# Head outputs turned inside the next weight block, and the first weight block of the heads rounded by two engines

## The reference, cut to what matters

```python
xn = rmsnorm(x, g_attn_norm)
z = einsum('bsd,de->bse', xn, w_in)           # queries, keys, values, gates of all branches
h_a, C, n, m = mlstm_branch(...)              # 8 heads, 128 query/key and 256 value channels each
h_b = attend(q_b, c_kv, k_rope)               # latent attention over 8 x 1024 cached rows
merged = sigmoid(gate_a) * (h_a @ w_branch_a) + sigmoid(gate_b) * (h_b @ w_branch_b)
x = x + merged @ w_out
out = x + conv_ffn(rmsnorm(x, g_ffn_norm), ...)
```

```python
num = sc @ v + w_state * (q @ C)
den = sum(sc) + w_state * (q @ n)
h = num / maximum(abs(den), exp(-m_row))
hid = rmsnorm(h) * g_out                      # over the head's 256 channels
h_a = hid * sigmoid(o_pre)
C_new = decay * C + k_weighted.T @ v
```

## Time and profile before

| | |
|---|---|
| median of 3 runs | 2805.84 us (2803.6 to 2806.14) |
| the profiled execution's own time | 2807.38 us |
| span of its instructions | 2805.5 us |
| TensorE matmuls busy | 2754.9 us, 98% of the span |
| VectorE, ScalarE, GpSimd busy | 58%, 46%, 14% |
| DMA | 393.54 MB, mean 140 GB/s |
| granted clock of TensorE, mean | 0.996 |

### The profile page before, as it was taken

How to read it: one execution, slowest core, us unless ns; L and a number is a source line. 1 busy time by engine, 2 the same in 40 slices (tenths; PEclk the granted TensorE clock), 3 DMA queues, 4 the chain that set the end, 5 groups by cost and what they waited for, 6 DMA issues and landing times.

```text
span 2805.5 us, 54137 instructions
## 1 busy us (share of the span) xinstructions
PE 2754.9 (98%) x19290; PEld 2617.0 (93%) x19290; DVE 1620.3 (58%) x2705; ACT 1299.6 (46%) x2333; POOL 401.8 (14%) x762
## 2 busy tenths in 40 slices
PE   8999899999999999999999999999999999999999
PEld 7865799999999988999999999999999999999999
DVE  4565866665566653555455344455777644677644
ACT  5536665555556543444453333344444433444433
POOL 0102343333334310000000000022000000000000
PEclk9999999999999999999999999999999999999999
DMA  6624112222222266565757555566555456555464
GB/s 193 240 69 106 37 38 59 63 51 57 52 62 52 53 217 204 168 205 158 214 151 208 164 166 165 162 185 177 164 162 165 144 168 183 165 164 165 141 186 124
DMA packets 697428, 393.54 MB, mean 140 GB/s; under 512 B 65304, under 2 KB 679394, under 8 KB 696296
## 3 DMA queue, kind: packets, MB, share of 16 engines
q1 hardware_dynamic: 685032, 378.64, 46.3%
q10 hardware_dynamic: 11824, 11.50, 1.2%
q0 software_dynamic: 368, 0.81, 0.1%
HBM read 368.13 MB, written 22.75 MB: 139 GB/s over the span
## 4 chain that ended last, share of the span: by engine, by line
PE 60%; DVE 1%; issue 1%; ACT 1%; ACTq 0%; DVEq 0%
PE bank L300 19%; PE bank L301 19%; PE bank L305 19%; PE bank L2672 0%; ACT sqm L2735 0%; PE bank L2650 0%; PE bank L2660 0%; DVE hn L2834 0%; PE bank L3181 0%; PE bank L2657 0%; PE bank L3224 0%; PE bank L2646 0%; DVE hn L2829 0%; ACT dws L2729 0%; DVE ns L2816 0%
## 5 line engine op out<-in xcount | busy, mean ns | idle before, releaser
L288 DVE TENSOR_TENSOR w_lo_b<-stage,w_hi_b 128x2048 fp32r<-128x2048 f32 (+1 forms) x289 | 619.0, 2142 | 405.6 <-ACT w_hi_b L281 405.5
L281 ACT ACTIVATE w_hi_b<-stage 128x2048 fp32r<-128x2048 f32 (+1 forms) x289 | 517.9, 1792 | 570.3 <-PE bank L305 531.1
L300 PE MATMUL bank<-xnH,w_hi_b 128*128 128x288 f32 x2752 | 747.2, 299 | 2.4 <-PEq L191 2.4
L301 PE MATMUL bank<-xnL,w_hi_b 128*128 128x288 f32 x2752 | 742.0, 296 | 0.0
L300 PEld LDWEIGHTS bank<-xnH,w_hi_b 128*128 128x128 f32 x2752 | 518.0, 188 | 12.1 <-issue 11.5
L301 PEld LDWEIGHTS bank<-xnL,w_hi_b 128*128 128x128 f32 x2752 | 517.5, 188 | 0.3
L1680 PE MATMUL bank<-uk_all,lat 128*128 128x384 f32 (+1 forms) x1344 | 446.1, 332 | 17.2 <-DVE lat L2466 5.8
L1682 PE MATMUL bank<-uk_all,lat 128*128 128x384 f32 (+1 forms) x1344 | 436.2, 325 | 0.0
L305 PE MATMUL bank<-xnH,w_lo_b 128*128 128x288 f32 x2752 | 391.9, 295 | 0.0
L305 PEld LDWEIGHTS bank<-xnH,w_lo_b 128*128 128x128 f32 x2752 | 373.8, 188 | 0.0
L1680 PEld LDWEIGHTS bank<-uk_all,lat 128*128 128x128 f32 x1344 | 254.6, 189 | 34.3 <-issue 23.9
(11 more groups left out here) (520 smaller groups left out, 3713.7 us busy)
## 6 DMA issues: line engine op xcount, KB each, us to landing
stage<-in_w_in_dram SPq DMA_DIRECT2D x88, 1024.0 KB, 5.2
stage<-in_w_up_dram SPq DMA_DIRECT2D x88, 1024.0 KB, 5.4
stage<-in_w_down_dram SPq DMA_DIRECT2D x64, 704.0 KB, 4.5
raw<-in_cache_kv_latent_dram SPq DMA_DIRECT2D x256, 64.0 KB, 1.8
stage<-in_w_branch_a_dram SPq DMA_DIRECT2D x16, 1024.0 KB, 5.7
stage<-in_w_branch_b_dram SPq DMA_DIRECT2D x16, 1024.0 KB, 5.5
stage<-in_w_out_dram SPq DMA_DIRECT2D x16, 1024.0 KB, 5.7
vals<-in_cache_kv_latent_dram SPq DMA_DIRECT2D x60, 256.0 KB, 3.0
```

The costliest lines, as they stand in the source:

```text
L281: act.activation(h, a, ACT.Copy).then_inc(w_hi, 1)
L288: dve.tensor_tensor(lo, a, h.bitcast(F32), ALU.subtract).then_inc(w_lo, 1)
L300: pe.matmul(out, hi, xH(k), start=first and k == 0, stop=False)
L301: pe.matmul(out, hi, xL(k), start=False, stop=False)
```

## The change

Two places are edited.

In the heads, step 3 of head h - 1 is no longer done after block 3 of body h. TensorE does it within block 4, between the 32 high products and the 16 low ones (`between`). ScalarE does its part of it after `split_hi` of block 5 (in iteration 4, ahead of `evac`), and VectorE after `split_lo` of block 5, ahead of step 4.

At the end of the page loop the first weight block is rounded by two engines: ScalarE copies the first half of its columns (chunks 0 to 7) and raises `w_hi`, VectorE the second half, between `sum21` and the last `norm_sum`, and raises the new `f_wh`. TensorE waits for `f_wh` ahead of chunk 8. The reload of the last chunk of `xnL` gets a semaphore of its own, `xn_last`, for which TensorE waits ahead of chunk 15 only.

```diff
-        def block(pe, n, z, xH, xL, width=P, kc=KC, first=True, last=True, ready=None):
+        def block(pe, n, z, xH, xL, width=P, kc=KC, first=True, last=True, ready=None, between=None):
...
                 pe.matmul(out, hi, xL(k), start=False, stop=False)
+            if between is not None:
+                between()
             need(pe, w_lo, n.of(1, 1))
...
+            first_raw, first_hi = stage[:, N0 % 4, :], ws["hi"][:, N0 % 2, :]
+            first_half, second_half = slice(0, KC * P // 2), slice(KC * P // 2, KC * P)
...
-                    reload(xnL, xnL_dram, 15, 16)
+                    reload(xnL, xnL_dram, 15, 16, xn_last)
...
                         for k in range(KC):
+                            if n == N0 and k == KC // 2:
+                                pe.wait_ge(f_wh, 1)
+                            if n == N0 and k == KC - 1:
+                                pe.wait_ge(xn_last, 16)
                             hi = ws["hi"][:, n % 2, k * P:(k + 1) * P]
...
-                    pe.wait_ge(xn_back, 112)
+                    pe.wait_ge(xn_back, 96)
                     block_high(N0)
...
                     act.wait_ge(k_p[4], upto(b, NG - 1))
-                    split_hi(act, At(N0))
+                    act.wait_ge(w_landed[N0 % 4], 16 * (N0 // 4 + 1))
+                    act.wait_ge(w_done, N0 - 1)
+                    act.activation(first_hi[:, first_half], first_raw[:, first_half], ACT.Copy).then_inc(w_hi, 1)
...
                     sum21(b, NG - 1)
+                    dve.wait_ge(k_p[4], upto(b, NG - 1))
+                    dve.wait_ge(w_landed[N0 % 4], 16 * (N0 // 4 + 1))
+                    dve.wait_ge(w_done, N0 - 1)
+                    dve.tensor_copy(first_hi[:, second_half], first_raw[:, second_half]).then_inc(f_wh, 1)
                     norm_sum(b, NG - 1, C21, 1, 0, e_q21, e_r21)
                     scale_a(b)
+                    dve.wait_ge(f_wh, 1)
                     split_lo(dve, At(N0))
...
+                        late = chain and j == 4
                         if blocks and not (h.i is None and h.c == 0 and j < 2):
-                            block(pe, n + j, n + j, lambda k: xnH[:, k, :], lambda k: xnL[:, k, :])
-                        if chain and j < 6:
+                            block(pe, n + j, n + j, lambda k: xnH[:, k, :], lambda k: xnL[:, k, :],
+                                  between=(lambda: step(h - 1, 3)) if late else None)
+                        if chain and j < 6 and j != 3:
                             step(h - 1, j)
-                pe.wait_ge(xn_back, 112)
+                pe.wait_ge(xn_back, 96)
+                pe.wait_ge(xn_last, 16)
...
                                 split_hi(act, n + (j + 1))
+                            if chain and j == 4:
+                                step(h - 1, 3)
...
-                        if chain and j < 6:
+                        if chain and j < 6 and j != 3:
                             step(h - 1, j)
...
                                 split_lo(dve, n + (j + 1))
+                        if chain and j == 4:
+                            step(h - 1, 3)
...
-                        if chain and j < 6:
+                        if chain and j < 6 and j != 3:
                             step(h - 1, j)
```

More of the change, by code:

```diff
@@ L1392, in head_load @@
             w_load(sp, At(N0 + 6 * h.c + m, 6 * h.step, h.i), w_in_v, h.of(mul, base))
-        xn_back = lasting("xn_back")
+        xn_back, xn_last = lasting("xn_back"), lasting("xn_last")
         nm_made, nm_out = lasting("nm_made"), lasting("nm_out")
@@ L1529, in build @@
             g_in, g_pe, g_act, g_cp, g_a, g_z, g_m, g_f = (sem("g_" + x) for x in ("in", "pe", "act", "cp", "a", "z", "m", "f"))
-            f_uv, f_hq, f_hq2 = sem("f_uv"), sem("f_hq"), sem("f_hq2")
+            f_uv, f_hq, f_hq2, f_wh = sem("f_uv"), sem("f_hq"), sem("f_hq2"), sem("f_wh")
+            first_raw, first_hi = stage[:, N0 % 4, :], ws["hi"][:, N0 % 2, :]
+            first_half, second_half = slice(0, KC * P // 2), slice(KC * P // 2, KC * P)
             q_tmp, q_add, q_hi, q_part = (sem("qs_" + x) for x in ("tmp", "add", "hi", "part"))
@@ L1638, in _, with reload @@
                     sp.dma_start(nm_dram, neg_MT[:]).then_inc(nm_out, 16)
-                    def reload(x, x_dram, c0, c1):
-                        sp.dma_start(x[:, c0:c1].bitcast(F32), x_dram[:, c0:c1]).then_inc(xn_back, 16)
+                    def reload(x, x_dram, c0, c1, done=xn_back):
+                        sp.dma_start(x[:, c0:c1].bitcast(F32), x_dram[:, c0:c1]).then_inc(done, 16)
                     sp.wait_ge(k_p[2], upto(b, NG - 3))
```

## The result

The changed kernel's median is 2813.54 us (12 runs, 2810.13 to 2815.43), beside 2807.14 us for the kernel before in 12 runs (2803.6 to 2811.04). The ratio is 1.0021, 95% interval 1.0013 to 1.0028: slower by 5.9 us, 3.6 to 7.9 us, by the ratio (the two medians differ by 6.4 us). The forecast was 2811.9 us, 6.1 us above the three runs known then. The profiled execution took 2813.89 us, its span is 2811.7 us.

What follows compares the result with a forecast made beforehand. TensorE was taken as the bound, its matmuls busy for 98% of the span, so the edits could only move gaps. +7.0 - 0.9 = +6.1 us on the 2805.84 us median gave 2811.9 us, 0.22% slower, range 2807 to 2815.

Steps and rivals of the forecast that it cites:

- likeliest case: Whole kernel: block 4 waits for its rounding in every head, costing more than the halved first rounding gains; 86%.
- edit 1: Heads: step 3 moved into block 4 costs 0.87 us a head, +7.0 us over 8 heads (5.4 to 8.5).
- edit 2: Page loop's end: first block rounded by two engines, -0.9 us (-0.4 to -2.2).
- the distance of the two ends: Heads: block 4's rounding ends 0.68 us after VectorE's scaling, in all 8; this is added to each head.
- From the semaphore to the first matmul: Heads, start of block 4: 0.05 to 0.25 us, taken as 0.15, hence 0.10 more than before.
- One more switch: Heads: step 3 between block 4's high and low products adds 0.0 to 0.2 us, taken as 0.09.
- Step 4 waits for nothing: Heads: `y` and `cpe` still come in time for step 4, covered by 0.4 us or more, no cost.
- The rest hangs on TensorE: Behind the page loop's gap: maxima, values and turning depend on TensorE and move with its earlier start.
- Rival 1: Heads: step 3's wait goes and block 4's weights are ready; gain 3.4 + 0.9 = 4.3 us, 2801.5 us; 9%.
- Rival 2: Heads: the clock falls in the new gaps of about 1.2 us, 11.2 us more, 2823 us; 5%.

Runs made afterwards that it cites:

- edit 2 alone: Changed kernel with step 3 put back behind block 3, only the first weight block's rounding halved between two engines: 2806.48 us, ratio 0.9993 to the kernel before.
- late rounding: Changed kernel with ScalarE rounding block 4 behind the copy of block 3's result: 2836.06 us, ratio 1.0098 to the kernel before.
- early rounding: Changed kernel with ScalarE rounding block 4 in iteration 2 instead of iteration 3 behind the root: 2802.66 us, ratio 0.9984 to the kernel before.
- edit 1 alone: Kernel before with only step 3 moved into block 4, page loop's end unchanged: 2811.79 us, ratio 1.0016.
- delayed rounding: Changed kernel with an unused 128 x 512 ScalarE copy between square root and block 4's rounding: 2818.81 us, ratio 1.0034 to the kernel before.
- edit 2 and all reloads awaited: Kernel before with the first block's rounding halved, TensorE still awaiting all seven reloads ahead of its first product: 2808.24 us, one run.

## Why the prediction was right

Its likeliest case is what happened, and the sum, +6.1 us, met a measured +5.9 us (3.6 to 7.9). That the two numbers are so close is in part luck: the interval is 4.3 us wide, edit 1 came out 0.9 us cheaper in the profile than forecast, and edit 2 is not resolved on the whole time. By its own steps:

- *Edit 1, the distance of the two ends*, 0.68 us: 0.69 us in the head shown; in the last head 1459.90 + 1.90 against 1460.24 + 0.88, 0.68 us. It is 0.68 or 0.69 us in all 8 heads of both profiles, as the prediction had argued from two.
- *From the semaphore to the first matmul*, taken as 0.10 us more than before: it is 0.05 us as before, so nothing more. The 0.25 us from which the upper end was taken belongs to the page loop's end, where after has it again (1036.71 + 1.06 = 1037.77 to 1038.03).
- *One more switch*, taken as 0.09 us: from the first matmul behind the gap to step 4 it is 1229.63 - 1221.32 = 8.31 us, where it was 1227.20 - 1218.95 = 8.25 us, so 0.06 us.
- Together 0.75 us in this head, 0.77 us in the mean, forecast 0.87. The size was 0.10 us too large, by the second term. Over 8 heads that is 0.8 us.
- *Step 4 waits for nothing*: so it was, with 1.3 us to spare. The estimate of at least 0.4 us had assumed that `yh` begins when step 3 is over; it begins 0.7 us earlier, behind the turning.
- *Edit 2*, -0.9 us (-0.4 to -2.2): from the start of the rounding to the first matmul it is 0.85 us less, where 0.86 was forecast. ScalarE's half took 1.06 us for 1.05. VectorE's half took 0.69 us, near the cheap end of 0.6 to 1.15. The landing of the load, which the sum held at its 1.42 us behind the last matmul, lay between 0.86 and 1.53 us and moved the gap with it. The clock, left open, went both ways: kept in after, lost in the kernel with edit 2 alone. Its price was put at 1.4 us; the prediction's own numbers, 12 x (0.25 - 0.14), give 1.3, and the profiles showed 1.4. Step and range hold; the value itself is below what the runs tell.
- *The rest hangs on TensorE*: not quite. Up to the second block 0.4 us were lost again, of which the wait for the maxima is 0.17, and the first body's load took back 1.0 us. Both waits come with the clock that held, not with edit 2's 0.85 us. Both terms were missing from the sum; in the range they had room.
- *Rival 1* fell because its condition did: the rounding had to be earlier. With the rounding earlier, its 3.4 us in the heads were 3.56.
- *Rival 2* did not come: the clock held in all 8 new gaps of 1.07 to 1.48 us. Its mechanism is real all the same, and came with the late rounding.

The Trainium skill, page "TensorE: Matmul & The Clock Gate", was cited in the prediction for ScalarE's strict order. The runs agree: a copy put ahead of the rounding moves it by the copy's whole 0.53 us, and only a change of the written order, in the early rounding, lets it pass the root.

What stays open: why the clock falls behind one gap and not behind another as long. Also, the stretch from the page loop's last matmul to the second body takes 57.0 to 59.9 us in the profiles with edit 2 and 59.0 to 60.3 us in those without it, depending on where the clock fell, so edit 2 cannot be priced closer than its interval.

## What to carry to other kernels

A wait can be hidden behind other work only if what comes to the front is ready: before moving an instruction that waits, look up when the inputs of its successor are complete, since a second end just behind the first is not shown by a list of waits. When two such ends stand close together, the reordering on the waiting engine and the earlier production on the other one have to be made as a pair; here each alone gained nothing or lost, and together they gained. A delay of 0.5 us put into both kernels is a cheap test of which end decides. When a gap begins with the wait for a load, measure an edit from the landing on, not over the whole gap.

## What the runs showed of the hardware

- *The clock behind gaps.* In the heads, 24 gaps of 1.07 to 2.00 us between the starts of two matmuls (after, edit 1 alone, delayed rounding) left the granted clock at 1.00; gaps of 2.73 to 2.79 us lowered it in 7 of 8 heads (late rounding). Length alone does not decide: in the middle of the page loop a gap of 2.29 us (662.26 to 664.55, idle for 1.96) lowered it in before and one of 2.30 us did not in the kernel with edit 2 and all reloads awaited; at the start of the heads a gap of 2.79 us kept it in after and lowered it at once in the kernel with the delayed rounding, and at the page loop's end a gap of 2.36 us kept it in after and one of 2.31 us in the kernel with the delayed rounding was followed by the low clock seven matmuls later. At the low level a matmul of 288 columns took 0.24 us, at the high one 0.13 us.
- *VectorE's rounding copy.* 128 x 1024 took 0.69 us (in after and with edit 2 alone), a subtraction of 128 x 2048 2.29 us: 0.67 and 1.12 ns a column. The Trainium skill, page "VectorE: DVE Perf Modes", section "Mode 2×_2P — use both read ports for one tensor", states that an operation with one source in SBUF can produce two results per cycle even in 32 bits, and one with two source tensors can't. The two durations agree with that if both have a fixed part of 0.16 us, which the subtractions of two widths give (128 x 1408 took 1.63 us: 0.66 us for 640 columns, 1.04 ns each, and 2.29 - 2048 x 1.04 ns = 0.16 us); for the copy, of which there is one width, it is taken over: (2.29 - 0.16) / 2048 = 1.04 ns, (0.69 - 0.16) / 1024 = 0.52 ns.
- *From semaphore to matmul.* TensorE started 0.05 us behind the end that released it in the heads, before and after, and 0.25 to 0.28 us behind it at the page loop's end, in the eleven profiles in which ScalarE's rounding held it. Why the second is longer was not tested.
